# Half of the gate-and-up tiles as Strassen products, and the feed-forward blocks in two chunks

## What is computed

```
def rmsnorm(x, g):
    inv = lax.rsqrt(jnp.mean(xf * xf, axis=-1, keepdims=True) + EPS)
    return (xf * inv) * g
def swiglu(h, wg, wu, wd):
    return (jax.nn.silu(h @ wg) * (h @ wu)) @ wd
for i in range(DEPTH):
    xp = xp + 0.5 * swiglu(rmsnorm(xp, norm_ffn1[i]), w_ffn1_gate[i], w_ffn1_up[i], w_ffn1_down[i])
    xp = xp + mixer(rmsnorm(xp, norm_mix[i]))
    xp = xp + 0.5 * swiglu(rmsnorm(xp, norm_ffn2[i]), w_ffn2_gate[i], w_ffn2_up[i], w_ffn2_down[i])
```

## Time and profile before

| | us |
|---|---|
| median of 3 runs (2511.92 to 2517.16) | 2516.29 |
| the profiled execution, its own time | 2512.74 |
| its span | 2511.0 |
| TensorE busy | 2449.6 |
| VectorE busy | 1158.5 |
| ScalarE busy | 869.6 |

### The profile page before, as it was taken

How to read it: one execution, slowest core, us unless ns; L and a number is a source line. 1 busy time by engine, 2 the same in 40 slices (tenths; PEclk the granted TensorE clock), 3 DMA queues, 4 the chain that set the end, 5 groups by cost and what they waited for, 6 DMA issues and landing times.

```text
span 2511.0 us, 48231 instructions
## 1 busy us (share of the span) xinstructions
PE 2449.6 (98%) x19185; PEld 2383.1 (95%) x19185; DVE 1158.5 (46%) x1772; ACT 869.6 (35%) x1638; POOL 5.3 (0%) x18
## 2 busy tenths in 40 slices
PE   8999999998999999989999999999999999999998
PEld 7999999865999999978999999999999999999998
DVE  5444334555555555535444434444434656444422
ACT  4222223463455555523222223222222223322211
POOL 0000000000000000000000000000000000000000
PEclk9999999999999999989999999999999999999999
DMA  4333333210211111202333233333333332333332
GB/s 135 88 90 91 93 90 113 87 42 21 57 38 49 44 43 46 57 17 76 92 92 92 86 93 90 93 91 92 88 93 90 93 93 85 93 92 92 88 93 72
DMA packets 372678, 198.85 MB, mean 79 GB/s; under 512 B 31168, under 2 KB 369174, under 8 KB 372552
## 3 DMA queue, kind: packets, MB, share of 16 engines
q1 hardware_dynamic: 372372, 197.03, 27.1%
q10 hardware_dynamic: 180, 0.11, 0.0%
HBM read 194.27 MB, written 2.87 MB: 79 GB/s over the span
## 4 chain that ended last, share of the span: by engine, by line
PE 93%; DVE 3%; ACT 2%; issue 1%; DMA 0%; SPq 0%; DVEq 0%; ACTq 0%; POOL 0%; POOLq 0%
PE ps L387 24%; PE ps L389 23%; PE ps L391 23%; PE ps L1339 15%; PE ps L1269 1%; PE ps L1172 1%; PE ps L1281 1%; PE ps L1272 1%; ACT sq L1611 1%; PE ps L1197 0%; DVE mxp L1241 0%; PE ps L1196 0%; PE ps L921 0%; PE ps L922 0%; PE ps L923 0%
## 5 line engine op out<-in xcount | busy, mean ns | idle before, releaser
L376 DVE TENSOR_TENSOR w_lo<-raw,w_hi 128x1024 fp32r<-128x1024 f32 (+2 forms) x328 | 391.7, 1194 | 887.3 <-ACT w_hi L370 887.1
L387 PE MATMUL ps<-h_hi,w_hi 128*128 128x260 f32 x3392 | 687.5, 284 | 10.3 <-DVE h_lo L410 6.2
L391 PE MATMUL ps<-h_hi,w_lo 128*128 128x260 f32 x3392 | 685.3, 284 | 0.0
L389 PE MATMUL ps<-h_lo,w_hi 128*128 128x260 f32 x3392 | 684.5, 283 | 0.0
L370 ACT CAST w_hi<-raw 128x1024 fp32r<-128x1024 f32 (+2 forms) x328 | 336.6, 1026 | 767.4 <-PE ps L391 753.7
L387 PEld LDWEIGHTS ps<-h_hi,w_hi 128*128 128x128 f32 x3392 | 525.4, 189 | 13.3 <-issue 6.3
L391 PEld LDWEIGHTS ps<-h_hi,w_lo 128*128 128x128 f32 x3392 | 525.0, 189 | 0.0
L389 PEld LDWEIGHTS ps<-h_lo,w_hi 128*128 128x128 f32 x3392 | 523.7, 189 | 0.0
L387 PE MATMUL ps<-g_hi,w_hi 128*128 128x260 f32 x1408 | 284.2, 283 | 0.0
L389 PE MATMUL ps<-g_lo,w_hi 128*128 128x260 f32 x1408 | 283.0, 282 | 0.0
L391 PE MATMUL ps<-g_hi,w_lo 128*128 128x260 f32 x1408 | 283.0, 282 | 0.0
(11 more groups left out here) (313 smaller groups left out, 2024.3 us busy)
## 6 DMA issues: line engine op xcount, KB each, us to landing
raw<-in_w_ffn_gate SPq DMA_DIRECT2D x88, 512.0 KB, 3.8
raw<-in_w_ffn_up SPq DMA_DIRECT2D x88, 512.0 KB, 3.8
raw<-in_w_ffn_down SPq DMA_DIRECT2D x64, 512.0 KB, 4.0
cache<-in_cache_latent SPq DMA_DIRECT2D x128, 128.0 KB, 2.0
raw<-in_w_ffn_down SPq DMA_DIRECT2D x32, 384.0 KB, 3.5
raw<-in_w_conv_in SPq DMA_DIRECT2D x24, 512.0 KB, 3.8
raw<-in_w_o_attn SPq DMA_DIRECT2D x8, 512.0 KB, 4.0
cache<-in_cache_krope SPq DMA_DIRECT2D x128, 32.0 KB, 1.8
```

Of the source, the lines that this page charges most:

```text
L376: nc.vector.tensor_tensor(w_lo[:, un.half, 0:n], src, w_hi[:, un.half, 0:n], ALU.subtract).then_inc(unit_lo_made, 1)
L387: nc.tensor.matmul(o[b], hi, mh[:, x0 + b * HALF:x0 + (b + 1) * HALF], start=start, stop=False)
L389: nc.tensor.matmul(o[b], hi, ml[:, x0 + b * HALF:x0 + (b + 1) * HALF], start=False, stop=False)
L391: mm = nc.tensor.matmul(o[b], lo, mh[:, x0 + b * HALF:x0 + (b + 1) * HALF], start=False, stop=stop)
```

## The change

In gate-and-up, tile 0 of a chunk of 11 tiles is done as before, then 5 pairs follow. The first tile of a pair is plain. The second is a two-by-two block product: the features in two halves of 4 blocks, the tokens in two halves of 260, and gate and up as the two rows of weights. Plain, that is 8 half products of 12 matmuls; here it is 7 (M1 to M7, `half_product`), each into one bank. Some need sums of weights (`first_sums`, `more_sums`, on VectorE, in `raw`) and sums of activations (`mix_hi`, `mix_lo`, four mixes for each of 4 k, made once per block by `mixes_act` and `mixes_dve`). Their results are put together by seven additions of 260 columns on VectorE.

The weights of a pair are split by halves: CG0, CG1 (plain gate), CU (plain up, two halves at once), M12 (two at once), M5, M4, M6, M3, M7. `SLOT_FREE` names the part whose use frees the place. ScalarE copies M1's result out of PSUM (`kept`).

Since the mixes take room, `g_hi` and `g_lo` hold one chunk of 11 tiles: a block does gate-and-up and down for chunk 0, adding half the sum to `xT` (counted by `x_part`, nothing published), then both for chunk 1. A down product has units of 4 and 7 blocks. The waits of SyncE for raw places follow the parts. Other edits join semaphores (`small_T`, `dve_consts`, `wu_in` and more) with the same waits as before, and unroll `down` for ScalarE and VectorE.

The diff, cut to its core. In order: constants, tiles, parts of a pair, mixes, half product, TensorE's loop and down, ScalarE, VectorE.

```diff
-DOWN = (8, 8, NF - 16)
+CHUNK = NF // 2
+DOWN = (4, CHUNK - 4)
+PAIRS = CHUNK // 2
+STEPS = 12
+ADDS = 7
+KH = KD // 2
+W = UC // 2
...
-            g_hi = sb("g_hi", [P, NF * T], F32R, m)
-            g_lo = sb("g_lo", [P, NF * T], F32R, m)
+            g_hi = sb("g_hi", [P, CHUNK * T], F32R, m)
+            g_lo = sb("g_lo", [P, CHUNK * T], F32R, m)
+            mix_hi = sb("mix_hi", [P, 4, KH, HALF], F32R, m)
+            mix_lo = sb("mix_lo", [P, 4, KH, HALF], F32R, m)
+            mix_f = sb("mix_f", [P, 2, 5, HALF], F32, m)
...
+        CG0, CG1, CU, M12, M5, M4, M6, M3, M7 = 0, 1, 2, 4, 6, 7, 8, 9, 10
+        LONG = {CU: 1, M12: 2}
+        SHORT = {CG0: (0, 0), CG1: (0, 1), M5: (3, 0), M4: (3, 1), M6: (3, 1), M3: (2, 1), M7: (2, 0)}
+        SLOT_FREE = {M12: CG1, M5: CU, M4: CU + 1, M6: M12, M3: M12 + 1, M7: M5}
+        SLOT_FREE_IN_PAIR_AHEAD = {CG0: M6, CG1: M3, CU: M7 + 1}
+        RAW_FREE = (CG1, CU + 1, M7 + 1, M3)
...
+        def part_hi(act, pr, q):
+            j = LONG[q] if q in LONG else SHORT[q][0]
+            pr.loaded(act, j)
+            if q >= M12:
+                act.wait_ge(part_used, pr.step(SLOT_FREE[q]))
+            elif pr.first:
+                act.wait_ge(unit_used, pr.uc + (2 if q == CU else 1))
+            else:
+                act.wait_ge(part_used, pr.step(SLOT_FREE_IN_PAIR_AHEAD[q] - STEPS))
+            if q in (M5, M6, M3, M7):
+                act.wait_ge(sums_made, 3 * pr.n + {M5: 1, M7: 1, M6: 2, M3: 3}[q])
+            if q in LONG:
+                nc.scalar.copy(part(w_hi, q, 2), raw[:, pr.raw_slot(j), :]).then_inc(part_hi_made, 2)
+            else:
+                nc.scalar.copy(part(w_hi, q), pr.raw_half(*SHORT[q])).then_inc(part_hi_made, 2 if q == M7 else 1)
+        def part_lo(dve, pr, q):
+            dve.wait_ge(part_hi_made, pr.step(q + (q in LONG or q == M7)))
+            if q in LONG:
+                nc.vector.tensor_tensor(part(w_lo, q, 2), raw[:, pr.raw_slot(LONG[q]), :], part(w_hi, q, 2),
+                                        ALU.subtract).then_inc(part_lo_made, 2)
+            else:
+                nc.vector.tensor_tensor(part(w_lo, q), pr.raw_half(*SHORT[q]), part(w_hi, q),
+                                        ALU.subtract).then_inc(part_lo_made, 2 if q == M7 else 1)
...
+            s = 2 * pr.raw_slot(2)
+            nc.vector.tensor_tensor(halves[:, s:s + 3:2, :], halves[:, s:s + 4:3, :],
+                                    halves[:, s + 2, :].unsqueeze(1).to_broadcast([P, 2, W]), ALU.add).then_inc(sums_made, 1)
...
+        def mix_sums(dve, n, at, k, step):
+            g = KD * GAIN[n] + k
+            f = mix_f[:, k % 2]
+            x0, x1 = k * T, (k + KH) * T
+            dve.wait_ge(mix_act, mix_act_count(at, k, 0))
+            step.link(nc.vector.scalar_tensor_tensor(out=f[:, 1, :], in0=f[:, 0, :], scalar=-1.0, in1=f[:, 4, :],
+                                                     op0=ALU.mult, op1=ALU.subtract))
+            nc.vector.scalar_tensor_tensor(out=f[:, 2, :], in0=xT[:, x0 + HALF:x0 + T], scalar=gain[:, g:g + 1],
+                                           in1=f[:, 4, :], op0=ALU.mult, op1=ALU.subtract).then_inc(mix_dve, 1)
+            nc.vector.scalar_tensor_tensor(out=f[:, 3, :], in0=xT[:, x1:x1 + HALF], scalar=gain[:, g + KH:g + KH + 1],
+                                           in1=f[:, 1, :], op0=ALU.mult, op1=ALU.add).then_inc(mix_dve, 1)
+        def mix_round(act, at, k):
+            act.wait_ge(mix_dve, mix_count(at, k, 1))
+            nc.scalar.copy(mix_hi[:, :, k, :], mix_f[:, k % 2, 0:4, :]).then_inc(mix_act, 1)
...
+        def mixes_act(act, n, at, ks):
+            for k in ks:
+                mix_base(act, n, at, k)
+            for k in ks:
+                mix_round(act, at, k)
+        def mixes_dve(dve, n, at, ks, step):
+            dve.wait_ge(x_ready, KD * (n + 1))
+            dve.wait_ge(gains_made, 1 + (n > 0))
+            for k in ks:
+                mix_diff(dve, at, k)
+            for k in ks:
+                mix_sums(dve, n, at, k, step)
+            for k in ks:
+                mix_rest(dve, at, k)
...
+        def half_product(bank, q, mh, ml):
+            hi, lo = part(w_hi, q), part(w_lo, q)
+            o = ps[:, bank, 0:HALF]
+            for k in range(KH):
+                kc = slice(k * P, (k + 1) * P)
+                nc.tensor.matmul(o, hi[:, kc], mh(k), start=k == 0, stop=False)
+                nc.tensor.matmul(o, hi[:, kc], ml(k), start=False, stop=False)
+                mm = nc.tensor.matmul(o, lo[:, kc], mh(k), start=False, stop=k == KH - 1)
+            return mm
...
+            with pe.Fori(0, PAIRS) as it:
+                pr = Pair(ch, it)
+                for j in range(2):
...
+                    for h in range(2):
+                        q = (CG0, CG1, CU, CU + 1)[2 * j + h]
+                        pe.wait_ge(part_lo_made, pr.step(q if j == 0 else CU + 1))
+                        hi, lo = part(w_hi, q), part(w_lo, q)
+                        for k in range(KH):
+                            kc = slice(k * P, (k + 1) * P)
+                            mm = product(2 + j, hi[:, kc], lo[:, kc], h_hi, h_lo, KH * h + k,
+                                         h == 0 and k == 0, h == 1 and k == KH - 1)
+                        mm.then_inc(part_used, 1)
+                pe.wait_ge(part_lo_made, pr.step(M12 + 1))
+                pe.wait_ge(hid_done, pr.t)
+                pe.wait_ge(gate_scaled, pr.t + 1)
+                half_product(4, M12, tokens(h_hi, 0, 0), tokens(h_lo, 0, 0)).then_inc(part_used, 1)
+                half_product(5, M12 + 1, tokens(h_hi, KH, 0), tokens(h_lo, KH, 0)).then_inc(part_used, 1)
+                pe.wait_ge(part_lo_made, pr.step(M5))
+                pe.wait_ge(mix_ready, KH * (at + 1))
+                half_product(0, M5, mix(mix_hi, 0), mix(mix_lo, 0)).then_inc(part_used, 1)
+                pe.wait_ge(part_lo_made, pr.step(M4))
+                half_product(1, M4, mix(mix_hi, 3), mix(mix_lo, 3)).then_inc(part_used, 1)
+                pe.wait_ge(part_lo_made, pr.step(M6))
+                half_product(2, M6, mix(mix_hi, 1), mix(mix_lo, 1)).then_inc(part_used, 1)
+                pe.wait_ge(part_lo_made, pr.step(M3))
+                half_product(3, M3, tokens(h_hi, KH, 1), tokens(h_lo, KH, 1)).then_inc(part_used, 1)
+                pe.wait_ge(part_lo_made, pr.step(M7 + 1))
+                pe.wait_ge(up_scaled, pr.t + 1)
+                half_product(6, M7, mix(mix_hi, 2), mix(mix_lo, 2)).then_inc(part_used, 2)
...
+                for j in range(8):
+                    m, p = j // 2, j % 2
...
+                        pe.wait_ge(hid_done, t0 + CHUNK - 1 + p)
+                        pe.wait_ge(added, ADDS * PAIRS * (ch + 1) + 1)
...
+            nxt = Pair(ch, 0)
+            if c == 0 and n:
+                mixes_act(act, n, at, (0, 1))
+                norm_act(act, n)
+            part_hi(act, nxt, CG0)
+            part_hi(act, nxt, CG1)
+            if c == 0 and n == 0:
+                norm_act(act, n)
+                mixes_act(act, n, at, (0, 1))
+            if c == 0 and n - 1 == CONV_NORM:
+                tails_act(act)
+            gate_silu(t0)
+            if c == 0:
+                mixes_act(act, n, at, (2, 3))
+            part_hi(act, nxt, CU)
+            def pair(it, last):
+                pr = Pair(ch, it)
+                round_hid(pr.t - 1, pr.f - 1)
+                part_hi(act, pr, M12)
+                gate_silu(pr.t)
+                part_hi(act, pr, M5)
+                part_hi(act, pr, M4)
+                round_hid(pr.t, pr.f)
+                act.wait_ge(part_used, pr.step(M12))
+                nc.scalar.copy(up_t[:, 0:HALF], ps[:, 4, 0:HALF]).then_inc(kept, 1)
+                part_hi(act, pr, M6)
+                part_hi(act, pr, M3)
+                part_hi(act, pr, M7)
+                if last:
+                    act.wait_ge(part_used, pr.step(M6))
+                    split_hi(act, Unit(uc + 2), DOWN[0] * P)
+                    gate_silu(pr.t + 1)
+                    act.wait_ge(part_used, pr.step(M7 + 1))
+                    split_hi(act, Unit(uc + 3), DOWN[1] * P)
+                    round_hid(pr.t + 1, pr.f + 1)
+                else:
+                    nxt = Pair(ch, it + 1)
+                    part_hi(act, nxt, CG0)
+                    part_hi(act, nxt, CG1)
+                    gate_silu(pr.t + 1)
+                    part_hi(act, nxt, CU)
...
+            nxt = Pair(ch, 0)
+            if c == 0 and n:
+                mixes_dve(dve, n, at, (0, 1), step)
+                norm_dve(dve, n)
+            part_lo(dve, nxt, CG0)
+            part_lo(dve, nxt, CG1)
+            if c == 0 and n == 0:
+                norm_dve(dve, n)
+                mixes_dve(dve, n, at, (0, 1), step)
+            if c == 0 and n - 1 == CONV_NORM:
+                tails_dve(dve)
+            dve.wait_ge(inv_made, ROW_USE[n] + 1)
+            dve.wait_ge(unit_used, uc + 1)
```

(61 more changed lines are left out.)

448 lines of the change are left out of this document (253 added, 195 removed).

## The result

| | before | changed |
|---|---|---|
| median of 13 runs | 2513.43 us (2511.02 to 2517.16) | 2525.24 us (2519.78 to 2528.38) |
| ratio of the times, 95% interval | | 1.0041 (1.0033 to 1.0050) |
| profiled execution | 2512.74 us, span 2511.0 | 2519.78 us, span 2518.0 |
| mean granted clock of the profiled one | 0.991 | 0.982 |

The change makes the kernel 0.4% slower, 11.8 us between the medians; the forecast was 2530, slower. One remark is needed for what follows: the profiled execution is the quickest of the 13, and the others show a mean granted clock of 0.978 to 0.982. So the trace explains 7.0 us (2518.0 less 2511.0), and the other 4.8 us lie in executions of the changed kernel that were not traced.

What follows compares the result with a forecast made beforehand. TensorE was taken to bound the kernel. Saving, ends, starts, clock after starts and clock after ends: -57.7 + 15 + 45.5 + 6 + 6 = +15 us, 2528 against the profiled 2512.74, median put at 2530; 8-in-10 range 2504 to 2548.

Steps and rivals of the forecast that it cites:

- saving, 480 matmuls: Gate-and-up pairs: 84 matmuls in place of 96 in each of 40 tiles, at 0.1202 us, saves 57.7 us.
- eight ends: End of each chunk: TensorE waits 1.9 us for VectorE's chain after M7, eight times, +15 us, bounds 12 to 19.
- start of block 0: First block's start: TensorE waits for CU's low part behind reciprocal and mixes, 15.1 less 0.4, so 14.7 us.
- start of block 2: Third block's start: mixes and norm stand ahead of the first pair's parts on VectorE, costing 10.0 us.
- clock after the starts: After each of four starts' waits of 3 us or more TensorE's clock falls, 1.5 us each, +6 us.
- clock after the ends: At chunk ends: half of the eight waits, just under 2.20 us, lose the clock, +6 us, bounds 0 and 12.
- The loop: Pair loop: bound by TensorE at 21.6 us, VectorE busy about 17.7, with 1.0 us to spare at the worst place.
- The start chain: Block starts: VectorE's and ScalarE's in-order mixes, norm and splits delay TensorE, 45.5 us over four starts, bounds 38 to 54.
- The second waits of the later blocks: Sign at block starts: after a wait for `w_lo` of about 5 us, a second of 3 to 5.
- the loop bound by VectorE: Pair loop: TensorE waits for CU in each of 32 pairs, 1 us a pair, 2562 us; chance 0.12.
- The short start: Block starts cost 7 us each, 30 in all, and the ends' 1.5 us waits keep the clock; 2504 us, chance 0.22.
- The holding clock: Clock holds through all ends and costs nothing after starts; +3, 2519 us; chance 0.18 with what lies near it.

Runs made afterwards that it cites:

- the eighth half product: Changed kernel with half product M7 done twice in each of the 40 pairs, 480 matmuls more; 2575.77 us.
- the reordered starts: Changed kernel with block starts reordered: splits not needing norm or mixes earlier, two of four mixes behind the first direct tile's arithmetic; 2507.26 us.
- no mixes: Changed kernel without computing the four activation mixes; half products read split activations instead, with as many matmuls; 2476.47 us.

## Why the prediction was right, and where it wasn't

The sum of the profiled execution, in the prediction's own terms; "start" counts both waits and what the clock loses between them, above the 48 matmuls (5.77 us) of CG0 and CG1:

| term | predicted | measured |
|---|---|---|
| saving, 480 matmuls | -57.7 | -57.2 (8 x 7.15, from the eighth half product) |
| eight ends | +15 | +14.0 (8 x 1.75) |
| start of block 0 | +14.7 | +14.7 (15.11 - 0.4) |
| start of block 1 | +10.2 | +10.2 (5.74 + 1.71 + 2.78) |
| start of block 2 | +10.0 | +10.2 |
| start of block 3 | +10.6 | +10.6 (6.23 + 2.55 + 2.48 - 0.66) |
| clock after the starts | +6 | +5.4 |
| clock after the ends | +6 | 0 |
| sum | +15 | +8 (the spans differ by 7.0; the attention stage came out 1.0 shorter) |

The clock after the starts is the time from the last wait of a start to the chunk's end, less the 876 matmuls in it at 0.1202 (105.3): 106.49, 106.69, 106.61 and 106.79 us, so 1.2 to 1.5 each.

**The loop** was read rightly: nothing inside it waits, and the pair is 21.6 us, of which VectorE is busy for 17.6 where 17.7 were worked out. **The start chain** was the strongest part. In the third block the forecast put the end of `mix_lo` 6.8 us behind the start of the last `acc` and the end of CU's split 23.4 behind it; the rows have 7.0 (1560.91 + 2.46 - 1556.36) and 23.7. The second waits of the later blocks came out at 2.48 to 2.87 us, under the 3 to 5 that were named as a sign: the low clock behind the first wait stretched the 48 matmuls between the two by 1.6 to 2.6 us, and VectorE ended the second wait at the same time all the same. Only the wait of 3.85 us that block 0 would keep without mixes was not seen as a floor. **The ends** were 0.15 too long each.

**The clock at the ends** is the step that failed: it was priced at +6 and cost nothing. Of eight waits "just under 2.20" half were taken to lose the clock, on the evidence of one fall after 2.20 us, and in the profiled execution none did. In five traces (the changed kernel twice, the eighth half product, the reordered starts, no mixes) all 40 ends of 1.74 to 1.75 us kept 1.00, and all eight of 2.84 lost it. That the median came near the forecast all the same is luck: a usual execution is 4.8 us longer than the profiled one against the kernel before, for a reason that the prediction doesn't have. Part of that may be at the ends. Without their 14.0 us of waits the medians fell by 17.6 and, with the starts reordered, by 16.4 (2507.26 less 2490.89), but these medians are known to some 3 us each, so 14.0 alone may be all of it. Where the traces run the same work, they differ ahead of the first block's products (the row with 2.20 us of wait starts at 20.1 to 22.7), in the attention stage (753.2 to 762.4) and by one fall of the clock at a start (1.3, with the eighth half product). Which waits lose the clock in the executions near 2525 stays open.

**The median.** Predicted 2530, measured 2525.2. Of the 5 us, 2.9 is the base: the median of before was 2516.29 in three runs and 2513.43 in thirteen. From the sum's +15 to the measured +11.8 are 3.2 more, and the forecast had been rounded down by 1.3 from 2516.29 + 15.

Of the rivals, the loop bound by VectorE fell with the eighth half product. The short start (7 us each) fell with the waits as they stand. The holding clock was half right: it held at the ends and fell at the starts. Of the forecast's terms the loop, the ends and the starts came true by their mechanism.

The Trainium skill (TensorE: Matmul & The Clock Gate, HAM oscillation) describes a loop whose waits of some 3 to 5 us lower the clock every time. The prediction carried that over to all eight ends, whose waits are shorter; here those of 1.75 us lost no clock, those of 2.84 us each did.

## What to carry to other kernels

A form of the product with fewer multiplications moves its cost to where the loop isn't: what it needs ready ahead of the first tile and what it finishes after the last. Write down the in-order row of the helper engine for those two places, since here a saving of 57.7 us in the loop was lost to four starts and eight ends whose sum could be worked out from durations to within 1 us. Both can be largely had back by order alone: put what the first tile can do without the new operands ahead of them, and other ready work between the last tile and its reader; that turned 1.0041 into 0.9906. And read a wait in several executions before the clock behind it is priced: one fall after 2.20 us was the whole evidence for the term that failed, and in five of eleven traces the clock held behind that same wait.

## What the runs showed of the hardware

GpSimd and VectorE lengthen each other when both do elementwise work between SBUF tensors: a 1024-column subtraction on VectorE took 2.81 us where it takes 1.22 alone, `g_lo` 1.51 where it takes 0.69, and a 260-column one on GpSimd 1.62 where it takes 0.75. `gate_t` (0.69), which has one input in PSUM, and the reciprocal (3.40), which has a single input, took as long as ever beside it. I had expected it to be idle help; the rival on this was stated without a price. The Trainium skill (GPSIMD Engine Reference, Specifications) says that GpSimd shares VectorE's way to SBUF and that they contend where a VectorE instruction has two inputs there; the rows agree, with up to 2.3 times the duration. The shape of it is a wait rather than a slower pace. The two remainders on GpSimd ran from 1562.39 to 1564.85 and from 1564.93 to 1567.67; `g_lo` beside the first ended 0.55 us behind it, and the split beside the second 1.08 behind it, nearly their whole 0.69 and 1.22. The factor therefore holds for these lengths alone. So moving two of four mixes to the idle engine gained 1.4 us of 2491, within the spread.
